# A streaming encoder step with a mixture of experts on one core: first gathers, expert loop and final norm rearranged

## The reference, cut to what matters

```python
x = x + gate_m * mixed                      # "x2" in the kernel
h = rms_norm(x, gain) * (1 + scale_f) + shift_f   # "h2"
probs = softmax(h @ w_router)               # 16 experts in 4 groups
# one group of 4 is chosen, then the best 2 experts inside it; e_idx, w
for e in range(16):
    he = silu(h @ w_gate[e]) * (h @ w_up[e])     # 1024 -> 512
    y = y + gates[:, e:e+1] * (he @ w_down[e])   # 512 -> 1024
x = x + gate_f * y
out = rms_norm(x, final_norm_gain)
```

## Time and profile before

| what | us |
|---|---|
| median of 3 runs (lowest, highest) | 795.17 (790.38, 796.73) |
| the profiled execution | 793.92 |
| its span, first to last instruction | 792.2 |

### The profile page before, as it was taken

How to read it: one execution, slowest core, us unless ns; L and a number is a source line. 1 busy time by engine, 2 the same in 40 slices (tenths; PEclk the granted TensorE clock), 3 DMA queues, 4 the chain that set the end, 5 groups by cost and what they waited for, 6 DMA issues and landing times. The chain is left out here.

```text
span 792.2 us, 18875 instructions
## 1 busy us (share of the span) xinstructions
PE 685.7 (87%) x7369; PEld 440.3 (56%) x7370; DVE 375.0 (47%) x1063; ACT 207.7 (26%) x429; POOL 204.6 (26%) x338
## 2 busy tenths in 40 slices
PE   3699999999978889998799995699999899999925
PEld 1386476444334677665655553466667666666611
DVE  3200024101198788666644458245545454555536
ACT  4310037000242032367301110122323222232212
POOL 1212100100546520220100000243444444453410
PEclk9899999999989979999699997699999999999968
DMA  8963082535303110490293039789999999995063
GB/s 334 392 252 107 0 319 99 222 128 230 125 14 117 51 30 3 160 365 9 79 422 154 27 133 366 273 349 414 415 417 416 414 418 411 416 419 187 30 213 137
DMA packets 37541, 179.59 MB, mean 227 GB/s; under 512 B 5817, under 2 KB 6217, under 8 KB 21809
## 3 DMA queue, kind: packets, MB, share of 16 engines
q1 hardware_dynamic: 29536, 157.31, 50.3%
q0 software_dynamic: 7952, 21.55, 7.8%
HBM read 168.00 MB, written 13.71 MB: 229 GB/s over the span
## 5 line engine op out<-in xcount | busy, mean ns | idle before, releaser
L1756 PE MATMUL bank<-weights,x_hT 128*128 128x512 f32 x256 | 113.6, 602 | 0.0
L1740 PE MATMUL bank<-x_hT,weights 128*128 128x272 f32 x384 | 93.3, 405 | 2.3 <-DMA weights<-in_w_in 2.3
L2044 PE MATMUL bank<-weights,R 128*32 128x256 f32 x1408 | 83.0, 388 | 13.0 <-issue 6.6
L1740 PEld LDWEIGHTS bank<-x_hT,weights 128*128 128x128 f32 x384 | 75.1, 197 | 19.4 <-DMA weights<-in_w_in 2.7
L1756 PEld LDWEIGHTS bank<-weights,x_hT 128*128 128x128 f32 x256 | 48.9, 193 | 60.4 <-issue 60.2
L2044 PEld LDWEIGHTS bank<-weights,R 128*32 128x32 f32 x1408 | 54.3, 112 | 38.7 <-issue 13.1
L844 POOL DMA_INDIRECT y_d<-R,x_hT x44 | 45.1, 1024 | 101.9 <-DVE R L1601 49.0
L1084 ACT ACT_TABLE_LOAD x44 | 56.5, 1283 | 22.5 <-DVEq L1191 21.8
L1084 ACT ACTIVATE R<-bank 128x128 f32<-128x128 f32 x44 | 12.2, 277 | 184.8 <-PE bank L2044 184.8
L1565 DVE STREAM_TRANSPOSE R<-R 128x256 f32<-128x256 f32 x45 | 20.0, 445 | 85.4 <-PE bank L2044 85.4
L838 POOL DMA_INDIRECT R<-h_d,x_hT x46 | 49.5, 1075 | 37.6 <-POOL x_hT L856 21.8
(11 more groups left out here) (353 smaller groups left out, 994.2 us busy)
## 6 DMA issues: line engine op xcount, KB each, us to landing
weights<-in_w_ada SPq DMA_DIRECT2D x24, 1024.0 KB, 11.8
weights<-in_w_exp_gate SPq DMA_DIRECT2D x16, 1024.0 KB
weights<-in_w_exp_down SPq DMA_DIRECT2D x16, 1024.0 KB
weights<-in_w_exp_up SPq DMA_DIRECT2D x16, 1024.0 KB
R<-in_w_exp_down SPq DMA_DIRECT2D x16, 1024.0 KB
weights<-in_w_in SPq DMA_DIRECT2D x7, 2048.0 KB, 9.0
R<-in_w_exp_up SPq DMA_DIRECT2D x8, 1024.0 KB
R<-in_w_exp_gate SPq DMA_DIRECT2D x8, 1024.0 KB
```

The source lines that it names most:

```text
L1740: ins = T.matmul(bank[b][:, 0:HALF], w[:, k, h * P:(h + 1) * P], hT[:, k, c * HALF:(c + 1) * HALF], start=(n == 0), stop=(n == KT - 1))
L1756: ins = T.matmul(bank[b][:, :], hT[:, k, i * P:(i + 1) * P], w[:, k, :], start=(k == 0), stop=(k == KT - 1))
L2044: ins = T.matmul(bank[2][32 * j:32 * j + 32, 0:2 * P].rearrange("p (w f) -> p w f", w=2), XT[:, k, :], W2[:, :, k, j * P:(j + 1) * P], sta ...
```

## The change

- SP and POOL: x2 of all five blocks goes to DRAM and comes back for the end; PE's copy into PSUM and its adds at the end are gone. The eight small loads of `gateF` go ahead of some weight pieces. Weight pieces of experts 3 and 2 that followed the x2 wait now also wait until the first two gathers have landed (`s_gath`).
- Routing: `row_hot` has 32 columns instead of 128, the row numbers are multiplied into it (`row_entry`), the table has 32 rows and one column per tile; the copies for the other 96 partitions are made by four short instructions. MAXT is 64. A new semaphore `s_gseq` releases the first two gathers, which read their index column in place, ahead of `s_rd`.
- Expert loop: PE's code has all 16 experts one after the other; the two register loads of expert e+1 stand behind the first tile of expert e. DVE computes `factor` for a tile after the output of the tile before, not ahead of turning the hidden rows.
- The end: the outputs of each token's first expert (lower number) are loaded once all tiles of experts 0 to 14 are stored, and added to x2 before the last tile's outputs arrive; then those of the second expert. DVE makes all adds, one root for all five blocks; ACT scales two blocks and DVE three.

```diff
 @ sync
             filled(sp, "y31")
             first_pieces(0, (2, 3))
+            for gi in range(2):
+                for j in range(4):
+                    sp.dma_start(gateF[...], bcast(mod_d[...], 32)).then_inc(s_ph3, 16)
             first_pieces(1, (0, 1))
             first_pieces(3, (3,))
             filled(sp, "lg3")
             sp.wait_ge(s_h2, NTILE)
             first_pieces(1, (5, 4))
-            sp.wait_ge(s_x2w, 32)
-            sp.wait_ge(s_xsum, 1)
+            sp.wait_ge(s_x2w, 16 * NTILE)
+            both(sp, s_h2w)
+            for n in range(2):
+                sp.wait_ge(s_gath[n], 16)
             first_pieces(3, (2, 0, 1))
-            both(sp, s_h2w)
             first_pieces(2, (0,))
...
-            for i in (0, 4):
+            for i in range(NTILE):
                 sp.dma_start(xr[i][0:ROWS[i], :], x2_d[...]).then_inc(s_xr, 16)
...
+            done = sp.value_load(base_i[0:1, NE - 1:NE], min_val=2, max_val=MAXT)
+            sp.wait_ge(s_yd, done + 1)
+            for n in range(2):
+                stored = sp.value_load(base_i[0:1, NE + 3 + n:NE + 4 + n], ...)
+                sp.wait_ge(s_yst[n], stored * 16)
+            for i in range(NTILE):
+                sp.dma_start(yb[i][0:n, :], y_d[TOK + i * P:TOK + i * P + n, :]).then_inc(s_yb, 16)
...
-                sp.dma_start(yb[i][0:n, :], y_d[TOK + i * P:TOK + i * P + n, :]).then_inc(s_ya[i], 16)
 @ gpsimd
-                if i in xr:
-                    pool.wait_ge(s_x2, 2 * m + 2)
-                    pool.dma_start(x2_d[...], x[0:n, i, :]).then_inc(s_x2w, 16)
+                pool.wait_ge(s_x2, 2 * m + 2)
+                pool.dma_start(x2_d[...], x[0:n, i, :]).then_inc(s_x2w, 16)
...
-            pool.wait_ge(s_rd, 1)
-            later_pairs = pool.value_load(...)
             both(pool, s_h2w)
...
+            pool.wait_ge(s_gseq, 1)
             for n in range(2):
-                g.tensor_copy(gather_rows[n], tseq[:, n, 0:1]).then_inc(s_idx, 1)
-                pool.wait_ge(s_idx, n + 1)
-                gather(n)
+                gather(n, gseq[:, n:n + 1])
+            pool.wait_ge(s_rd, 1)
+            later_pairs = pool.value_load(...)
 @ scalar
+            act.wait_ge(s_root, 1)
+            for m in (0, 1):
+                A.activation(y, y, ACT.Identity, scale=st[0:n, 105 + m:106 + m]).then_inc(s_fin[m], 1)
 @ route (vector)
-            V.tensor_tensor(row_hot, iota_r..., [P, 2 * NTILE, P], ... ALU.is_equal)
-            vlink(dve, V.tensor_tensor(tile_hot, ... [P, 2 * NTILE, MAXT + 2] ...))
-            V.tensor_tensor(tile_entry, ... [P, 2 * NTILE, MAXT + 2, 2], ALU.mult).then_inc(s_oh, 1)
+            vlink(dve, V.tensor_tensor(row_hot, ... [P, 2 * NTILE, ET], ... ALU.is_equal))
+            V.tensor_tensor(row_entry, row_hot, entry... [P, 2 * NTILE, ET], ALU.mult)
+            V.tensor_tensor(tile_hot, ... [P, 2 * NTILE, MAXT + 2] ...).then_inc(s_oh, 1)
...
-            read("dve", "tab", V.tensor_scalar(tseq, tb, 4.0, quarter_out, ALU.mult, ALU.add))
+            vlink(dve, V.tensor_scalar(second, tab, float(-7 * TOK), float(-TOK), ALU.is_ge, ALU.mult))
+            vlink(dve, V.tensor_tensor(second, second, tab, ALU.add))
+            for j in range(P // ET):
+                ins = V.tensor_scalar(gseq[j * ET:(j + 1) * ET, :], second, 4.0, ...)
+            ins.then_inc(s_gseq, 1)
+            for j in range(P // ET):
+                ins = V.tensor_scalar(sseq[j * ET:(j + 1) * ET, :], tab, 4.0, ...)
+            read("dve", "tab", ins)
+            V.tensor_tensor(row_weight, row_hot, weights2...).then_inc(s_tg, 1)
...
             dve.sem_inc(s_rd, 1)
 @ vector
             for t in range(1, 5):
                 hidden(t)
-                gate_factors(t)
                 turn_hidden(t)
                 y_out(t - 1, (t - 1) % 2)
                 reorder_rows(t + 2, t % 2)
+                gate_factors(t)
...
+            for i in FIN:                       # FIN = [4, 0, 1, 2, 3]
+                V.tensor_tensor(xr[i], xr[i], yb[i], ALU.add)
+            for m, i in enumerate(FIN):
+                dve.wait_ge(s_ya[i], 16)
+                V.tensor_tensor(xr[i], xr[i], ya[i], ALU.add).then_inc(s_comb, 1)
+            for m in (0, 1):
+                V.tensor_tensor(ya[FIN[m]], xr[FIN[m]], fing, ALU.mult).then_inc(s_gain, 1)
+            dve.wait_ge(s_fsq, NTILE)
+            rstd(st[:, 105:110], st[:, 100:105], D)
+            for m in range(2, NTILE):
+                V.scalar_tensor_tensor(ya[i], xr[i], st[:, 105 + m:106 + m], fing, ALU.mult, ALU.mult)
 @ tensor
-            for i, places in psums.items():
-                for c, b in enumerate(places):
-                    ins = T.matmul(bank[b][:, :], ident[:, :], x[:, i, c * 512:(c + 1) * 512], ...)
-            ins.then_inc(s_xsum, 1)
...
-                nt = pe.value_load(ntile_i[0:1, bass.ds(e, 1)], ...)
-                base = pe.value_load(base_i[0:1, bass.ds(e, 1)], ...)
                 gate_up(par, base)
-                if not first:
+                if e:
                     down((par + 3) % 4, base)
                 for c in range(4, 6):
                     pe.wait_ge(s_we[par][c], loads_done)
+                following = counts(e + 1) if e + 1 < NE else None
                 with pe.Fori(1, nt) as i:
                     gate_up(par, base + i)
                     down(par, base + i)
-            for par in range(4):
-                expert(par, par, 16, first=(par == 0))
-            with pe.Fori(1, NE // 4) as four:
-                for par in range(4):
-                    expert(par, four * 4 + par, four * 16 + 16)
+            here = counts(0)
+            for e in range(NE):
+                here = expert(e, *here)
...
-            for i in FIN[2:]:                   # identity matmuls of ya and yb into PSUM, L2087
```

More of the change, by code:

```diff
@@ L279, in build @@
         grp("pos", 6, "dve")
-        grp("tab", 6, "dve")
-        grp("gates", 6, "dve")
+        grp("tab", TAB, "dve")
+        grp("gates", GATES, "dve")
         pe_done = sem("pe_done")
@@ L481, in build @@
         ntile_i = view(XH, 9100, NE).bitcast(I32)
[L482 to L487, removed]
+        base_i = view(XH, 9120, NE + 5).bitcast(I32)
+        gather_rows = [view(XH, 9144 + n, 1).bitcast(I32) for n in range(2)]
+        scatter_rows = [view(XH, 9146 + n, 1).bitcast(I32) for n in range(2)]
         dst = view(R, T0 + 1444, 2 * NTILE)
@@ L492, in build @@
         dst_t = view(R, T0 + 1056, 2 * NTILE)
[L494 to L499, removed]
+        entry = view(R, T0 + 1464, 2 * NTILE)
+        iota_r = view(R, T0 + 1484, ET)
+        iota_t = view(R, T0 + 1484 + ET, MAXT + 2)
+        gseq, sseq = (view(XH, 8960 + n * (MAXT + 2), MAXT + 2).bitcast(I32) for n in range(2))
+        row_hot = view(R, 1920, 2 * NTILE, ET)
+        row_entry = view(R, 2240, 2 * NTILE, ET)
+        row_weight = view(R, 2560, 2 * NTILE, ET)
+        row_index = view(R, 2880, MAXT + 2)
         tile_hot = view(R, 3200, 2 * NTILE, MAXT + 2)
-        tile_entry = view(R, 0, 2 * NTILE, MAXT + 2, 2)
+        xr = [view(W, n * D, D) for n in range(NTILE)]
         ya = [view(W, 6 * SLOT + n * D, D) for n in range(NTILE)]
@@ L506, in build @@
         factor = view(XH, 8192 + 2 * QD, QD)
[L507 to L511, removed]
+        fing = view(W, 5 * D, D)
+        jk = view(W, 6 * D, D)
+        FIN = [4, 0, 1, 2, 3]
         row_gate = view(R, 1920, 2, MAXT + 3)
-        s_ya = [sem(f"y_rows_in{i}") for i in range(NTILE)]
+        s_yb = sem("first_expert_rows_in")
+        s_ya = [sem(f"last_expert_rows_in{i}") for i in range(NTILE)]
         s_ph3 = sem("final_in")
@@ L1603, in _ @@
             filled(dve, "gates")
-            read("dve", "gates", V.tensor_copy(row_gate[:, :, 1:], bank[6][:, 0:2 * (MAXT + 2)].rearrange("p (g t) -> p g t", g=2)))
+            for j in range(P // ET):
+                ins = V.tensor_copy(row_gate[j * ET:(j + 1) * ET, :, 1:], bank[GATES][0:ET, 0:2 * (MAXT + 2)].rearrange("p (g t) -> p g t", g=2))
+            read("dve", "gates", ins)
             taken(dve, "gates")
@@ L1997, in _ @@
             router(4, 1)
-            pe.wait_ge(s_x2, 2 * NTILE)
-            for i, places in psums.items():
-                for c, b in enumerate(places):
-                    taken(pe, last[b])
-                    ins = T.matmul(bank[b][:, :], ident[:, :], x[:, i, c * 512:(c + 1) * 512], start=True, stop=False)
-            ins.then_inc(s_xsum, 1)
             begin("pos")
@@ L2020, in _ @@
             for j in range(2 * NTILE):
-                ins = T.matmul(bank[6][:, 0:2 * (MAXT + 2)], row_hot[:, j, :], tile_entry[:, j, :, :].rearrange("p t c -> p (t c)"),
+                ins = T.matmul(bank[TAB][0:ET, 0:MAXT + 2], row_entry[:, j, :], tile_hot[:, j, :],
                                start=(j == 0), stop=(j == 2 * NTILE - 1))
@@ L2029, in _ @@
                 for j in blocks:
[L2030 removed]
```

(1 more changed line is left out.)

180 lines of the change are left out of this document (76 added, 104 removed).

## The result

The changed kernel took 783.41 us (median of 4 runs, 782.24 to 785.9) against 795.03 for the kernel before (790.38 to 796.73): ratio 0.9877, 95% interval 0.9827 to 0.9926. It is faster by 11.6 us or 1.2%, about half of the 22 that the prediction gave. The profiled execution took 784.38 us, with a span of 782.6, which is 9.6 less than before.

The account below looks back on a forecast made before the run. The prediction took the time as three parts in a row: routing and first gather, PE's own expert-loop stream, and the end. Gains of 7.5 + 5.8 + 8 = 21.3 us from 793.9 gave 772.6, median 773; range 761 to 785.

Parts of the forecast that it names:

- start: Routing and first gather: gather issued 3.3 us earlier and taking 2.4 us instead of 7.28; 7.5 us gained in all.
- loop: PE's expert boundaries: straight code cuts 15.9 us of gaps to fourteen of 0.72 us, 10.1 in all; 5.8 us gained.
- the End: Last scatter's landing to span's end: half the loads and adds done earlier, 24.8 us instead of 32.9; 8 us gained.
- slow "pos": Routing on PE: the matmul group before "tab" may run at 1.2 GHz after idling; costs 0.5 us.
- the gather is slow for another reason: Rival at the first gather: weights are not what slows it; start gives 2.6 to 4.4 us, time 777; chance 0.1.
- The hold costs nothing: Weight stream: pieces delayed until the first gathers land still leave 7 us of room at expert 12, so PE never waits.
- Loads hide: Rival in the expert loop: register loads run under queued matmuls, boundaries vanish, 15.9 us gained; time 765; chance 0.2.
- the loop gives nothing: Rival in the expert loop: loop exit and loads stall at two places, no gain; time 780; chance 0.1.
- Instruction fetch: Slower rival: PE's straight code for experts 4 to 15 waits on busy DMA engines, losing 88 us; time 861; chance 0.03.

Follow-up runs that it names:

- first pair: Profiles of the kernel before and of the changed kernel from the first measurement; changed kernel 783.41 us against 795.03, ratio 0.9877.
- second pair: Both kernels profiled again, unedited, on one chip; spans 790.2 and 775.2 us, changed kernel's median 777.22 us, ratio 0.9776.
- the adds held: Changed kernel, with DVE's five early adds made to wait until POOL has issued the last scatter: 774.15 us, ratio 0.9716.
- without the hold: Changed kernel, with SP's wait for the first two gathers before the weight pieces taken out: 780.65 us, ratio 0.982.
- the loop alone: Kernel before, with only PE's straight 16-expert code and moved register loads taken from the changed kernel: 787.6 us, one execution.

## Why the prediction was wrong, and where it was right

The terms, from the profiles (gain in us; the second pair had a nearly equal first part):

| term | forecast | first pair | second pair (790.2 to 775.2) |
|---|---|---|---|
| first part | 0 | -5.9 | 0.6 |
| start, up to the second tile | 7.5 | 5.3 | 7.2 |
| loop | 5.8 | 5.5 | 2.6 |
| scatter's landing | 0 | -5.0 | -5.0 |
| landing to the end | 8 | 9.5 | 9.6 |
| sum, with 0.2 and 0 ahead of the scatter | 21.3 | 9.6 | 15.0 |

In the first pair 11.7 us are missing: 5.9 in the first part, 5.0 in the scatter's landing, 2.2 in the start and 0.3 in the loop, less 1.5 that the end gave more than forecast and 0.2 ahead of the scatter.

**The step that failed** is the End's. It counted from the last scatter's landing and took the landing itself as unchanged at 2.36 us. It put the early adds "while PE works", but in DVE's stream they stand behind the last tile's output, so they ran beside POOL's last scatter (751.20 to 756.95 us), which they held: it landed after 7.33 us, 5.0 later. With that the End gave 4.5 instead of 8, inside the bounds of 3 to 12, but by another mechanism than any the prediction had. From the landing on it gave 9.5, 1.5 more than forecast: loads and adds took 9.6 us instead of 11.2, the stores behind the last scaling 5.4 instead of 5.0. With the adds held, which puts part of them on the path, it gave 8.8 (32.86 to 24.0).

**The size that no term had.** Another 5.9 us of the shortfall in the first pair came ahead of the first store that the change adds on POOL. The prediction compared with a profile whose first part ended at 468.67 us and took that for a constant. Over the series the changed kernel's runs lie from 776 to 786 us, and those of before from 790 to 802. The series had ratios of 0.9877, 0.9776 and 0.9801: the first one's four runs all lie in the upper half of that spread. PE's longer work, which the lower clock goes with, is 5.6 of the 7.2 us between the changed kernel's two profiles, but only 2.2 of the 5.9 of the first pair. Why the granted clock falls in some executions and not in others was not tested, and what made the other 3.7 us of the first pair stays open. So the forecast's 21.3 us were never measured as a sum: the nearest is 15.0, in the second pair.

**Start: right in mechanism, the gather mis-sized.** Counted from the first part's end, the gather went out 2.75 us earlier in the first pair and 3.7 in the second (forecast 3.3 less 0.5 for the slow "pos"). The gather itself took 2.9 to 3.0 us in three profiles and 4.1 to 5.0 in the four others with the hold as it is, not 2.4: the scatter of the same rows was too low a price. In the three, the second gather landed 1.4 to 2.8 us after the first, in the others both landed together; why is open. So the hold gave 4.9 us, as forecast, only in the best case (7.82 to 2.95); in the first pair the gather gained 2.3 (7.28 to 5.00), which is why the start gave 5.3 and not 7.5. The rival that the gather is slow for another reason is refuted for 2.8 to 4.9 of its 7.8 us. The Trainium skill (DMA: Bandwidth & Descriptors, Latency and other measured facts) puts an HBM access at 0.2 us on average and 2 us at high load, from which the prediction's estimate of the weights' share was some 1.8 us; the profiles show 2.3 to 4.9.

**"The hold costs nothing": wrong, at expert 15.** The prediction let the stream go 4 us forward, since expert 4's pieces "follow without the pause", and so kept 7 us of room at expert 12. Without the hold the stream does go forward: expert 13's first pieces are issued at 659.47 us, 3.4 before the 662.85 of the earlier trace rows. With it they are issued at 662.76 in the second pair's changed kernel, where they stood before. The hold takes back what the stream had gained, while PE comes forward: the distance at expert 12, 14.9 us before, is 9.5 without the hold and 2.0 with it. By expert 15 it is used up in three profiles, those with the gathers apart: PE waited for weights at expert 15 for 1.9, 1.2 and 1.0 us, with the held pieces issued 1.9, 1.5 and 0.5 us after PE's first matmul. Where they were issued 0.6 us ahead of it, or earlier, it did not wait. In the second pair this is 1.9 of what the loop lacks to 5.8; the rest is that the kernel before ran its loop in 232.07 us in that profile, not 233.5.

**Loop: right in place, near in size.** 5.5 us in the first pair for 5.8, though the second profile of before, which ran its loop 1.4 us faster, leaves 4.0 to the straight code; 14 gaps of 0.4 to 0.7 us ahead of the second tiles, none ahead of the first. "Loads hide" is refuted by the gaps, "the loop gives nothing" by the loop alone (228.08 us). Instruction fetch, the slower rival, showed no stall: in the changed kernel's first profile the gaps are 0.44 to 0.72 us in experts 4 to 14 and 0.41 to 0.57 in experts 1 to 3, though the page of the profile counts 50 packets of instructions for 0.82 MB (38 and 0.62 before).

One sum in the prediction is off by a microsecond: 772.6 and 1.25 make 773.9, not 773. Nothing hangs on it.

## What to carry to other kernels

Before work is moved "under" another engine's wait, look at what every engine does in that window, not only at the path's: elementwise adds moved ahead of a last scatter's landing cost about half of what the two halves had won (5.0 of 10.8 us), and one semaphore gave back about 4 of it. Work can move under a wait only as far as its own engine's stream lets it. A transfer that is held back in a saturated stream is paid for where the stream is closest to its consumer, which may be the last stage and not the one with the smallest room in the old trace. A forecast of a few per cent needs more than one execution of before: where an untouched stretch varies by 10 us, the terms are to be checked between profiles in which it agrees.

## What the runs showed of the hardware

- While DVE ran five float32 adds of 1,024 columns with both operands in on-chip memory, POOL took 5.96 us for one indirect DMA, and the DMA engines moved nothing until the adds had ended; alone, or beside DVE's smaller operations in the loop, it took 0.98 to 1.07. The Trainium skill (GPSIMD Engine Reference, Specifications) says that the two engines share their interface to that memory and collide on DVE instructions with two such inputs. The trace agrees that they collide, 5.96 us against 0.99; that it is this interface was not tested by itself.
- A gather of 128 rows of 1 KB took 2.9 to 5.0 us with no transfer beside it but the gather of the next tile, and 6.7 to 7.8 us under the weights (three profiles of the kernel before or its start, and the run without the hold); the scatter of as many rows took 2.4 with nothing beside it.
- In straight code PE stood idle for 0.4 to 0.9 us ahead of the tile behind two register loads, and the gap moved with them from an expert's second tile to its first, also with a whole `down` queued in front of them. In the hardware loop the boundary cost 0.7 to 1.4 us.
